# A two-block layer on one core: sixteen buffers for expert tiles instead of twelve, and the filter, its spectra and the embedding product inside the expert stage

## The chip, the core and the metric

The kernel runs on one core of a Trainium2 chip. The metric is the device time of one execution in microseconds (us). TensorE (PE in the profile) multiplies, VectorE (DVE) and ScalarE (ACT) compute elementwise and bring results out of PSUM, GpSimd (POOL) does a few tiny operations, and SyncE (SP) issues nearly all transfers. The engines run their own instruction streams and wait for one another by semaphores.

## The reference

`x` is 256 tokens by 1024 channels. The reference is two blocks, one after the other:

```python
# block 1
x = x + hybrid_mixer(rms_norm(x), ...)          # state space mixer and attention
x = x + hier_moe(rms_norm(x), ...)              # 32 experts, 2 of them for each token
gate = sigmoid(rms_norm(x) @ w_ple_gate)        # 1024 x 1024
x = x + gate * (p @ w_ple)                      # p: 256 x 256, w_ple: 256 x 1024
x = rms_norm(x)
# block 2
proj = rms_norm(x) @ w_in_2                     # hyena branch, attention branch, gates
k_spec = hyena_filter_spectra(L, w_f1, ..., w_f3)   # depends on weights and positions only
...                                             # long convolutions with k_spec, attention
x = x + merged @ w_out_2
```

and of it

```python
def hier_moe(...):          # per expert, d = 1024, f = 256
    hid = silu(h @ w_gate[e]) * (h @ w_up[e])
    out += comb[:, e] * (hid @ w_down[e])
def hyena_filter_spectra(...):
    h = sin(freq_1 * (z @ w_f1 + b_f1)); h = sin(freq_2 * (h @ w_f2 + b_f2))
    k = (h @ w_f3) * decay                      # 256 x 2048
    return rfft(concat(k[:, :, 0], k[::-1, :, 1]))
```

`p @ w_ple` and `k_spec` depend on nothing that is computed before them.

## The kernel before

**Dense products.** The weights of the dense products come as tiles of up to 128 x 2048 words (1 MB) through four raw buffers (`raw`). ACT copies a tile into a high part (`WH`, L1022), DVE subtracts it from the raw tile for a low part (`WL`, L1438), in three slots each, and PE multiplies high and low parts in three passes (`gemm`, `mul3`). Every PE product is issued by one of two helpers, L469 (`mul`) and L478 (`turn`, a transpose), so nearly all PE rows carry these lines. A product of float32 operands shows as two matmul rows in the profile, one of the split kind as one row each pass.

**The expert stage.** The 32 experts are done four at a time, in eight rounds `q` = 0 to 7. Each round has twelve tiles of 1 MB: four `w_gate`, four `w_up`, four `w_down`, 96 in all. They are not split but used as float32. PE does in a round, in this order: `first(q, 0)` (gate, 32 products that go to four column strips of one PSUM bank), `first(q, 1)` (up), `slots`, for q < 6 two gathers of token rows for the next pair of rounds, `scatter(q - 1)`, `hidden_T`, `down(q)`. The outputs are scaled (ACT L1259, DVE L1958) and the scatter adds them to four PSUM banks that stay open through the stage. With the two banks of `down` that leaves two of the eight banks (`ring.of`) for everything else in the stage. `Ring.take` makes PE wait, before it writes a bank again, for the engine that reads the bank's last contents.

**Buffers of the stage.** The tiles go to twelve buffers in turn (`held`): the four raw buffers, the six halves of the `WH` and `WL` slots, a part of `arena`, and `XN`. Tile t + 12 is fetched into the buffer of tile t as soon as the whole set of four that tile t belongs to has been multiplied (`fetch_expert`). All fetches stand in one queue, SP's, in the order in which the program writes them, and an entry that waits holds up everything behind it. After the first twelve tiles SP issues the constants of block 2 (`cst2`, 1952 KB; `w_f3_2`, 512 KB; two small matrices; `p`, 256 KB; the final norm's weight, 512 KB), then tiles 12 to 95, then the tiles of the dense weights `w_ple` (2 of 0.5 MB), `w_ple_gate` (4) and block 2's.

**The filter.** Its two small layers run at the ends of rounds 2 and 3. The eight products with `w_f3_2` (`kf`, 64 rows deep, 512 columns; DVE multiplies each by the decay, L1926) run four at the end of round 6 and four at the end of round 7. The spectra (eight steps `ks`, two float32 products of 128 x 128 x 512 each) are filler work after the stage: steps 0 and 1 after the product with `w_ple`, 2 and 3 after the transposes of the next norm, 4 to 7 after the product with `w_ple_gate`. Two steps make a pair: ACT copies the first one's bank, and DVE forms the difference and the sum with the second (L1485 or L1487, L1490).

**After the stage.** DVE splits the first three weight tiles, adds the scattered sums to `X` (L1982), and PE transposes `p`, multiplies it by `w_ple` (24 split products), transposes the normed `X` (`rows_T("np")`), multiplies by `w_ple_gate` (96 split products). The result is gated and added, two norms follow, `rows_T("ng")`, and block 2's products.

Of the kernel before, what the change touches and what calls it, by code (L numbers as in the profile page):

```python
# [12 lines left out]
ALU = mybir.AluOpType  # L13
# [6 lines left out]
NRAW = 4  # L20
# [4 lines left out]
NEXP = 12  # L25
# [139 lines left out]
def program(nc, A, out):  # L165
    ctx = ExitStack()
    with ctx:
# [8 lines left out]
        d_expert = [signal(f"d_e{i}") for i in range(NEXP)]  # L176
# [105 lines left out]
        iota, hyb = C["iota"], arena[0:1, 4096:5120]  # L282
# [21 lines left out]
        KI = arena[:, 6144:8192].rearrange("p (f d) -> p f d", f=2)  # L304
        PX = arena[:, 8192:10240].rearrange("p (t d) -> p t d", t=2)
# [5 lines left out]
        FH = arena[0:64, 10240:10752].rearrange("p (a l) -> p a l", a=2)  # L311
        PT_ = tuple(x[:, 0:512].rearrange("p (c l) -> p c l", c=2) for x in HD_)
        SG = sg_[:, :].rearrange("p (a l) -> p a l", a=2)
        FGU = arena[:, 4096:8192].rearrange("p (c n) -> p c n", c=8)
        FD = arena[:, 8192:10240].rearrange("p (c n) -> p c n", c=2)
# [9 lines left out]
        KQ = arena[:, 8192:9728].rearrange("p (t d) -> p t d", t=2)  # L325
        V2 = arena[:, 9728:10752].rearrange("p (t d) -> p t d", t=2)
# [61 lines left out]
        filled_from = dense_again % NRAW  # L388
        slots_in_order = [(dense_again + i) % NSPLIT for i in range(NSPLIT)]
# [3 lines left out]
        moe_set = lambda t: (("gate", "up", "down")[t // 4 % 3], t // 12)  # L393
        slot_emptied = {s: moe_set(96 - NEXP + NRAW + 2 * i + 1) for i, s in enumerate(slots_in_order)}
        for key, w, kc in (("wpl", wpl, 2), ("wpg", wpg, 8)):
            for i in range(2):
                weight((key, i), w, kc, 512 * i, 512)
# [31 lines left out]
        class Splitting:  # L429
# [5 lines left out]
            def due(self, consumed):  # L435
                while self.k < self.end:
                    before = tiles[self.k]["before"]
                    if before is not None and before >= consumed:
                        return
                    self.k += 1  # L440
                    yield self.k - 1
# [22 lines left out]
        def tensor(e):  # L464
# [34 lines left out]
            def fill(n):  # L499
                for name, c in todo.next(n):  # L500
                    if name == "spectra":
                        spectrum(c)
                        continue
# [234 lines left out]

            def first(q, m):
                if m == 0:  # L740
# [1626 lines left out]
```

## Time and profile before

| | us |
|---|---|
| median of three runs | 935.06 (933.81 to 940.55) |
| the profiled execution | 934.24, span 932.4 |
| PE busy | 777.8 (83% of the span) |
| DVE busy | 473.8 (51%) |
| ACT busy | 333.8 (36%) |
| expert tiles on their way | from 323 to 606 of the span |

The span is the part of the execution between the first and the last recorded instruction; the 1.8 us left are outside it. The page gives the engines' busy shares in 40 slices of 23.3 us; the chain of waits says what ended last, step by step.

### The profile page before, as it was taken

The page shows a single profiled execution, that of the slowest core. Times are in us where ns is not written, and L with a number is a line of the kernel's source. Part 1 is how long each engine was busy: PE and PEld are TensorE (multiplying, and loading weights), DVE is VectorE, ACT ScalarE, POOL GpSimd, SP SyncE. Part 2 cuts the span into 40 slices and gives each one's busy share as a digit, 9 for nine tenths or more (in the row PEclk, how much of TensorE's full clock was granted, in tenths as well). Part 3 has the DMA queues.
Part 4 walks back from the last instruction along what each step waited for, and adds up shares of the span by engine and source line. Part 5 has one row for each costly group of instructions (what it writes and reads, how often), then busy time and mean ns, then how long its engine had stood idle before and what let it go on. Part 6 is the DMA issues. An engine that isn't in the chain of part 4 may idle for free.

```text
span 932.4 us, 10988 instructions
## 1 busy us (share of the span) xinstructions
PE 777.8 (83%) x4611; PEld 583.8 (63%) x4611; DVE 473.8 (51%) x797; ACT 333.8 (36%) x485; POOL 20.3 (2%) x16
## 2 busy tenths in 40 slices
PE   3999799979989984677776676769799989999978
PEld 3988677757768873533343342337499866578766
DVE  5678755554675555311212111255575668755662
ACT  5454344545543235111101010034445452346620
POOL 0000000000000000000000000000000004100000
PEclk8999899889999998789888998879999999999999
DMA  7645551122442448699999999962236663242401
GB/s 255 199 171 187 174 181 46 46 91 90 136 136 82 156 153 339 227 422 420 421 422 421 420 421 421 415 230 90 69 99 203 199 209 115 68 158 91 135 1 45
DMA packets 62890, 190.30 MB, mean 204 GB/s; under 512 B 7633, under 2 KB 11955, under 8 KB 50356
## 3 DMA queue, kind: packets, MB, share of 16 engines
q1 hardware_dynamic: 61826, 187.01, 54.1%
q10 hardware_dynamic: 1010, 2.54, 0.7%
q8 instruction: 38, 0.62, 0.3%
q14 instruction: 16, 0.13, 0.0%
HBM read 188.49 MB, written 1.05 MB: 203 GB/s over the span
## 4 chain that ended last, share of the span: by engine, by line
PE 60%; DMA 18%; DVE 12%; ACT 6%; SPq 2%; issue 1%; POOL 0%; DVEq 0%; ACTq 0%
PE pb L469 58%; DMA WLo<-in_w_exp_up 14%; DVE WL L1438 3%; DMA XN<-in_w_exp_down 3%; ACT WH L1022 3%; PE pb L478 2%; SPq L2278 1%; DMA arena<-in_b_short 1%; ACT arena L1052 1%; DVE cv_ L1560 1%; SPq L2262 0%; ACT arenao L1225 0%; DVE arena L1502 0%; ACT L1052 0%; DVE XN L1445 0%
## 5 line engine op out<-in xcount | busy, mean ns | idle before, releaser
L1438 DVE TENSOR_TENSOR WL<-raw,WH 128x2048 fp32r<-128x2048 f32 (+5 forms) x82 | 176.5, 2166 | 124.7 <-ACT WH L1022 124.6
L469 PE MATMUL pb<-WH,HTh 128*128 128x512 f32 (+2 forms) x464 | 189.9, 409 | 22.3 <-DVE HTl L1465 7.8
L1022 ACT ACTIVATE WH<-raw 128x2048 fp32r<-128x2048 f32 (+5 forms) x82 | 147.1, 1805 | 150.8 <-PE pb L469 150.8
L469 PE MATMUL pb<-WH,HTl 128*128 128x512 f32 (+2 forms) x464 | 181.5, 391 | 0.0
L469 PE MATMUL pb<-WL,HTh 128*128 128x512 f32 (+2 forms) x464 | 181.5, 391 | 0.0
L469 PEld LDWEIGHTS pb<-WH,HTh 128*128 128x128 f32 x464 | 89.1, 192 | 48.5 <-issue 7.7
L469 PEld LDWEIGHTS pb<-WL,HTh 128*128 128x128 f32 x464 | 88.9, 192 | 18.3
L469 PEld LDWEIGHTS pb<-WH,HTl 128*128 128x128 f32 x464 | 89.3, 192 | 16.8 <-issue 1.2
L1941 DVE TENSOR_TENSOR rt_<-rt_,pb 128x256 f32<-128x256 f32 x8 | 3.4, 421 | 122.7 <-ACT rt_ L1249 122.7
L469 PE MATMUL pb<-arena 128*128 128x512 f32 (+6 forms) x188 | 63.1, 469 | 3.0 <-DVE arena L1926 2.2
L469 PE MATMUL pb<-WLo,arena 128*32 128x256 f32 x256 | 45.9, 498 | 19.4 <-DMA WLo<-in_w_exp_up 19.4
L469 PE MATMUL pb<-WHo,arena 128*32 128x256 f32 x256 | 48.0, 501 | 12.4 <-DMA WHo<-in_w_exp_up 12.4
L469 PE MATMUL pb<-raw,arena 128*32 128x256 f32 x512 | 41.2, 432 | 16.1 <-DMA raw<-in_w_exp_gate 15.0
L469 PE MATMUL pb<-HTh,WH 128*128 128x256 f32 (+1 forms) x184 | 53.4, 290 | 0.3 <-DVE HTl L1469 0.3
L469 PE MATMUL pb<-HTh,WL 128*128 128x256 f32 (+1 forms) x184 | 53.0, 288 | 0.0
L469 PE MATMUL pb<-HTl,WH 128*128 128x256 f32 (+1 forms) x184 | 53.0, 288 | 0.0
L1249 ACT ACTIVATE rt_<-pb 128x256 f32<-128x256 f32 x8 | 3.1, 383 | 126.9 <-PE pb L469 126.9
L469 PE MATMUL pb<-arena,rt_ 128*128 128x64 f32 (+1 forms) x160 | 43.5, 415 | 5.8 <-DVE rt_ L1475 5.8
L469 PEld LDWEIGHTS pb<-arena 64*128 64x128 f32 (+4 forms) x188 | 30.5, 191 | 26.8 <-issue 18.5
L469 PEld LDWEIGHTS pb<-WLo,arena 128*32 128x32 f32 x256 | 19.9, 141 | 43.2 <-DMA WLo<-in_w_exp_up 26.0
L469 PEld LDWEIGHTS pb<-raw,arena 128*32 128x32 f32 x512 | 19.2, 124 | 38.9 <-DMA raw<-in_w_exp_gate 20.2
L478 PE MATMUL pb<-c,arena 128*128 128x128 f32 (+2 forms) x200 | 28.9, 281 | 13.5 <-DMA arena<-in_b_short 4.7
(308 smaller groups left out, 1180.9 us busy)
## 6 DMA issues: line engine op xcount, KB each, us to landing
raw<-in_w_in SPq DMA_DIRECT2D x46, 1024.0 KB, 5.1
raw<-in_w_exp_gate SPq DMA_DIRECT2D x32, 1024.0 KB, 20.4
WHo<-in_w_exp_up SPq DMA_DIRECT2D x16, 1024.0 KB, 16.9
WLo<-in_w_exp_up SPq DMA_DIRECT2D x16, 1024.0 KB, 19.3
raw<-in_w_out SPq DMA_DIRECT2D x8, 1024.0 KB, 5.4
WHo<-in_w_exp_down SPq DMA_DIRECT2D x8, 1024.0 KB, 16.8
WLo<-in_w_exp_down SPq DMA_DIRECT2D x8, 1024.0 KB, 18.9
arena<-in_w_exp_down SPq DMA_DIRECT2D x8, 1024.0 KB, 20.6
```

The source lines that it names most:

```text
L469: return e.matmul(o, l, r, start=start, stop=stop, skip_group_check=True)
L478: return e.transpose(o, i, ident[0:k, 0:k])
L1022: e.activation(h_, r_, ACT.Copy).then_inc(hi.sem, hi.mark(k))
L1052: e.activation(dst[:, t, :], pb((name, t))[:, 0:n], f).then_inc(ac.sem, ac.mark((name, t)))
L1249: e.activation(HG[q % 2], pb(("gu", q))[:, 0:256], ACT.Silu).then_inc(ac.sem, ac.mark(("su", q)))
L1438: e.tensor_tensor(l_, r_, h_.bitcast(F32), ALU.subtract).then_inc(lo.sem, lo.mark(k))
L1560: e.scalar_tensor_tensor(out=cv[:, s:L], in0=u[:, 0:L - s], scalar=cw[:, 3 - s, g:g + 1], in1=cv[:, s:L], op0=ALU.mult, op1=ALU.add).then_inc(
L1941: e.tensor_tensor(HG[q % 2], HG[q % 2], pb(("gu", q))[:, 256:512], ALU.mult).then_inc(ve.sem, ve.mark(("gu", q)))
L2278: e.dma_start(held[i], w).then_inc(d_expert[i].sem, d_expert[i].mark(("x", t), by=16))
```

## The change

- **Sixteen buffers** for the first tiles (`NHELD`). Four of them, parts of `arena`, hold one tile each only (buffers 0, 1, 5, 7); from tile 16 on twelve buffers turn, and three of those (6, 9, 10) are given up during round 6. Which tile goes where is worked out ahead by a small table.
- The first sixteen tiles and tiles 16 to 27 stand in SP's queue **before** the constants of block 2, `p`, the final norm's weight and, new there, `hy_bias_2`, which ACT issued in round 5.
- `w_ple` is one float32 tile more in the stage's stream (97 tiles), ahead of round 7's. `p` is transposed at the end of round 2. The product is eight float32 products (`side_product`) at the start of round 7, two for each half of the columns and each half of the tokens, on the two free banks.
- All eight `kf` products stand at the end of **round 5**, and all eight steps of the spectra at the end of **round 6**. ACT's and DVE's part of them moves along.
- The weights' tiles start with `w_ple_gate`. The first of them is split by ACT after round 7 and by DVE inside the norm, between its sum and its scaling; the next two after the norm's high and low parts.
- The fallback for tokens that no slot takes uses other addresses; it is not entered.

The core of the diff:

```diff
-NEXP = 12
+NHELD = 16
...
-        held = ([raws[(filled_from + i) % NRAW] for i in range(NRAW)] + [x[:, s, :] for s in slots_in_order
-                for x in (WHf, WLf)] + [arena[:, 8192:10240], XN.rearrange("p t d -> p (t d)")])
+        held = [arena[:, 16896:18944], arena[:, 10752:12800], *last_raw[0:3], arena[:, 12800:14848],
+                arena[:, 8704:10752], arena[:, 14848:16896], last_raw[3],
+                *[x[:, s, :] for s in emptied for x in (WHf, WLf)], XN.rearrange("p t d -> p (t d)")]
+        held_once, held_until = (0, 1, 5, 7), {6: 79, 9: 81, 10: 82}
+        moe_tiles = []
+        for q in range(8):
+            moe_tiles += [("wpl",)] if q == 7 else []
+            moe_tiles += [(m, q, g) for m in ("gate", "up", "down") for g in range(4)]
+        ring, buffer_of, held_before, held_last = deque(), {}, {}, {}
+        for t, name in enumerate(moe_tiles):
+            i = t if t < NHELD else ring.popleft()
+            buffer_of[name], held_before[name] = i, held_last.get(i)
+            held_last[i] = name
+            if i not in held_once and t < held_until.get(i, len(moe_tiles)):
+                ring.append(i)
...
@@ tensor
+            def kernel_rows(n):
+                o = ring.take(("kf", n), ve)
+                ac.wait_ge(e, ("fh", 1))
+                mul(o[:, :], FH[:, 1, (n // 4) * 128:(n // 4) * 128 + 128],
+                    FW[:, (n % 4) * 512:(n % 4) * 512 + 512]).then_inc(mm.sem, mm.mark(("kf", n)))
...
+            def side_product(i, t):
+                o = ring.take(("px", i, t), (ve, ac)[t])
+                ac.wait_ge(e, "pT")
+                w = held_tile(("wpl",), 2)
+                for c in range(2):
+                    ins = mul(o[:, :], PT_[:, c, t * 128:t * 128 + 128], w[:, c, 512 * i:512 * i + 512], c == 0, c == 1)
+                ins.then_inc(mm.sem, mm.mark(("px", i, t), *([("wpl",)] if i and t else [])))
...
             for q in range(8):
-                first(q, 0)
-                first(q, 1)
+                if q == 7:
+                    for i in range(2):
+                        for t in range(2):
+                            side_product(i, t)
+                first(q, "gate")
+                first(q, "up")
...
-                if q >= 6:
-                    for n in range(4 * (q - 6), 4 * (q - 6) + 4):
...
+                if q == 5:
+                    for n in range(8):
+                        kernel_rows(n)
+                if q == 6:
+                    for s in range(8):
+                        spectrum(s)
...
-            for i in range(2):
-                gemm(("wpl", i), ("wpl", i), PT_, "pT", (ve, ac))
-            fill(2)
             rows_T("np")
-            fill(2)
             for i in range(2):
                 gemm(("wpg", i), ("wpg", i), HT, "np", (ac, ac))
-            fill(99)
             rows_T("ng")
...
@@ vector
-            def norm_rows(n, src):
+            def norm_rows(n, src, split_to=None):
                 norm_sum(n, src)
+                if split_to:
+                    weights(None, split_to)
                 po.wait_ge(e, ("rs", n))
...
@@ sync
-            for t in range(NEXP):
-                fetch_expert(t)
-            mm.wait_ge(e, ("mT", "T", 6))
-            ve.wait_ge(e, ("x mix", 1))
+            for t in range(28):
+                fetch_held(t)
+            mm.wait_ge(e, ("up", 0))
             e.dma_start(c2[:, 0:A["cst2"].shape[1]], A["cst2"]).then_inc(d_c2.sem, d_c2.mark("in", by=16))
...
-            for t in range(NEXP, 96):
-                fetch_expert(t)
+            for t in range(28, len(moe_tiles)):
+                fetch_held(t)
```

PE's instructions from the end of `down(6)` on (names `pb0` to `pb7` are PSUM banks; `arena` holds the filter's rows; `raw`, `WHo`, `WLo`, `XN` hold expert tiles). Before, two of the round's `kf` products run freely, the other two wait, and round 7 follows:

```order
L469 MATMUL pb6<-arena,rt_ 32x512
L469 MATMUL pb6<-XN,rt_ 32x512
L469 MATMUL pb7<-arena 128x512
L469 MATMUL pb0<-arena 128x512
L469 MATMUL pb7<-arena 128x512 [waits s_ve]
L469 MATMUL pb0<-arena 128x512 [waits s_ve]
```

With the change, in the same place:

```order
L485 MATMUL pb6<-WHo,rt_ 32x512
L485 MATMUL pb0<-arena 128x512 x2
L485 MATMUL pb7<-arena 128x512 x2
L485 MATMUL pb0<-arena 128x512 [waits s_ve]
L485 MATMUL pb0<-arena 128x512
L485 MATMUL pb7<-arena 128x512 x2
...
L485 MATMUL pb0<-WLo,arena 128x512 [waits d_e12,s_ve]
L485 MATMUL pb0<-WLo,arena 128x512
L485 MATMUL pb7<-WLo,arena 128x512 x2
L485 MATMUL pb0<-WLo,arena 128x512 [waits s_ve]
L485 MATMUL pb0<-WLo,arena 128x512
L485 MATMUL pb7<-WLo,arena 128x512 [waits s_ac]
L485 MATMUL pb7<-WLo,arena 128x512
L485 MATMUL pb0<-WHo,arena 32x256 [waits d_e13,s_ve]
```

Four pairs of spectra steps, each after the first with a wait for DVE, and the eight products with `w_ple` (its tile in `WLo`) now stand between `down(6)` and the first product of round 7.

SP's queue from the first tiles on, before:

```order
L2278 DMA arena<-in_w_exp_down 128x2048 [waits s_ve]
L2278 DMA XN<-in_w_exp_down 128x2048 [waits s_ve,s_mm]
L2313 DMA arena<-in_cst 128x3904
L2317 DMA arena<-in_w_f_2 64x2048
...
L2318 DMA arena<-in_final_norm_w 128x1024
L2278 DMA raw<-in_w_exp_gate 128x2048 [waits s_mm]
```

and with the change:

```order
L2313 DMA XN<-in_w_exp_gate 128x2048 [waits s_ve,s_mm]
L2313 DMA raw<-in_w_exp_up 128x2048 [waits s_mm]
L2313 DMA raw<-in_w_exp_up 128x2048
L2313 DMA raw<-in_w_exp_up 128x2048 [waits s_mm]
L2313 DMA arena<-in_w_exp_up 128x2048
...
L2313 DMA XN<-in_w_exp_gate 128x2048
L2348 DMA arena<-in_cst 128x3904
L2352 DMA arena<-in_w_f_2 64x2048
```

The constants stood behind tile 11, the first one into `XN`; now they stand behind tile 27, the second one into `XN`, which waits for round 1's gate products.

DVE at the norm after the stage, before:

```order
L1441 TENSOR_SCALAR small<-small 128x2 [waits s_ve,s_ac]
L1454 TENSOR_SCALAR XN<-X,small 128x1024 [waits s_po]
L1438 TENSOR_TENSOR WL<-raw,WH 128x2048 [waits s_hi]
L1475 COPY arena<-pb 128x512 [waits s_mm]
L1438 TENSOR_TENSOR WL<-raw,WH 128x2048 [waits s_hi]
```

and with the change:

```order
L1469 TENSOR_SCALAR small<-small 128x2 [waits s_ve,s_ac]
L1466 TENSOR_TENSOR WL<-raw,WH 128x2048 [waits s_hi]
L1484 TENSOR_SCALAR XN<-X,small 128x1024 [waits s_po]
L1499 SCALAR_TENSOR_TENSOR HTl<-pb,small,HTh 128x256 [waits s_ac]
```

One tile's split moved ahead of the scaling; the other splits, the copies and the spectra's sums left this place.

## Rows read from the trace of the kernel before

**Rows 1.** The page: tenths of full clock and of DMA time, 40 slices.

```profile
PEclk8999899889999998789888998879999999999999
DMA  7645551122442448699999999962236663242401
```

**Rows 2.** Busy time in stretches: us, PE, PEld, DVE, ACT, POOL, PEclk, DMA share, GB/s.

```profile
380.00:390.00 10.00, 7.90 (x62) 7.16 (x64) 3.42 (x8) 3.18 (x5) 0.00 (x0) 0.68 0.49 120
540.00:580.00 40.00, 28.83 (x259) 14.45 (x251) 5.31 (x16) 3.72 (x8) 0.00 (x0) 0.91 1.01 421
```

**Rows 3.** The chain that ended last: start, us, what (L469 is any product).

```profile
542.58 23.78 DMA WLo<-in_w_exp_up
566.40 5.75 PE pb L469 x58
...
576.36 3.69 PE pb L469 x32
...
581.99 24.23 DMA XN<-in_w_exp_down
606.26 3.63 PE pb L469 x26
```

**Rows 4.** Instructions of SP's queue in order of time: start, us, line, operation.

```profile
371.29 0.43 SPq L2313 DMA_DIRECT2D arena<-in_cst  x1
...
392.27 1.99 SPq L2278 DMA_DIRECT2D raw<-in_w_exp_gate  x4
...
404.37 0.33 SPq L2278 DMA_DIRECT2D WHo<-in_w_exp_down  x1
```

**Rows 5.** A DMA issue line: count, KB each, median us from issue to landing.

```profile
raw<-in_w_out SPq DMA_DIRECT2D x8, 1024.0 KB, 5.4
```

**Rows 6.** Matmuls in order of time, rounds 0, 6 and 7: start, us, shapes.

```profile
388.55 3.66 PE L469 MATMUL pb<-raw,arena 128*32 128x256 f32 x64 [1.08 <-DVE arena L1918]
...
579.93 1.98 PE L469 MATMUL pb<-arena 64*128 64x512 f32 x4
582.91 1.12 PE L469 MATMUL pb<-arena 64*128 64x512 f32 x2 [1.00 <-DVE arena L1926]
584.29 2.06 PE L469 MATMUL pb<-arena 64*128 64x512 f32 x2 [0.26 <-DVE arena L1926]
```

**Rows 7.** A stretch as in Rows 2, at half clock.

```profile
584.33:591.16 6.83, 6.83 (x50) 2.80 (x54) 1.87 (x3) 0.00 (x0) 0.00 (x0) 0.50 1.01 422
```

**Rows 8.** Matmuls in order of time, after the stage.

```profile
632.52 3.59 PE L469 MATMUL pb<-arena 128*128 128x512 f32 x8
635.95 1.94 PE L478 MATMUL pb<-c,XN 128*128 128x128 f32 x16
...
663.07 7.03 PE L469 MATMUL pb<-arena 128*128 128x512 f32 x16
```

**Rows 9.** ACT in order of time, after the stage.

```profile
641.49 0.60 ACT L1064 ACTIVATE arena<-pb 128x512 f32<-128x512 f32 x1 [1.83 <-PE pb L469]
```

**Rows 10.** The same view of DVE.

```profile
610.70 1.41 DVE L1958 SCALAR_TENSOR_TENSOR HDl<-pb,small,HDh 128x512 fp32r<-128x512 f32 x2 [6.67 <-ACT HDh L1259]
...
615.39 4.55 DVE L1438 TENSOR_TENSOR WL<-raw,WH 128x1024 fp32r<-128x1024 f32 x3
619.86 2.48 DVE L1982 TENSOR_TENSOR X<-pb,X 128x512 f32<-128x512 f32 x4
624.63 0.69 DVE L1465 TENSOR_TENSOR HDl<-pb,HDh 128x512 fp32r<-128x512 f32 x1 [2.30 <-issue]
625.24 1.22 DVE L1445 CUSTOM_DVE_ANT_0 XN<-X 128x1024 f32<-128x1024 f32 x1
...
627.56 0.75 DVE L1454 TENSOR_SCALAR XN<-X,small 128x1024 f32<-128x1024 f32 x1 [0.81 <-POOL small L2234]
632.00 2.29 DVE L1438 TENSOR_TENSOR WL<-raw,WH 128x2048 fp32r<-128x2048 f32 x1 [3.69 <-ACT WH L1022]
...
642.85 0.69 DVE L1490 TENSOR_TENSOR arena<-arena,pb 128x512 f32<-128x512 f32 x1
```

More of the change, by code:

```diff
@@ L1 @@
 import math
+from collections import deque
 from contextlib import ExitStack, nullcontext
@@ L439, in due, with until @@
                         return
+                    self.k += 1
+                    yield self.k - 1
+            def until(self, n):
+                while self.k < n:
                     self.k += 1
@@ L1012, in scalar, with weights @@
             todo = Steps()
-            def weights(consumed):
-                for k in splitting.due(consumed):
+            def weights(consumed, end=None):
+                for k in splitting.until(end) if end else splitting.due(consumed):
                     h_, _, r_ = tile_flat(k)
@@ L1247, in scalar @@
             for q in range(8):
+                if q == 7:
+                    for i in range(2):
+                        mm.wait_ge(e, ("px", i, 1))
+                        e.activation(PX[:, 1, 512 * i:512 * i + 512], pb(("px", i, 1))[:, :], ACT.Copy).then_inc(
+                            ac.sem, ac.mark(("px", i, 1)))
                 mm.wait_ge(e, ("up", q))
@@ L1263, in scalar @@
                     e.activation(FH[:, 1, :], FH[:, 0, :], ACT.Sin).then_inc(ac.sem, ac.mark(("fh", q - 2)))
-                if q == 5:
-                    e.dma_start(hyb, A["hy_bias_2"].rearrange("a o n -> a (o n)")).then_inc(
-                        d_hyb.sem, d_hyb.mark("in", by=16))
+                if q == 2:
+                    mm.wait_ge(e, "pT")
+                    e.activation(PT_, pb("pT")[:, :].rearrange("p (c l) -> p c l", c=2), ACT.Copy).then_inc(
+                        ac.sem, ac.mark("pT"))
+                if q == 6:
+                    for c in range(1, 8, 2):
+                        _, _, o_, _ = SPECTRA[c]
+                        mm.wait_ge(e, ("ks", c))
+                        e.activation((KR, KI)[c // 4][:, 0, o_ * 512:o_ * 512 + 512], pb(("ks", c - 1))[:, :],
+                                     ACT.Copy).then_inc(ac.sem, ac.mark(("ks", c)))
             splitting.end = len(tiles)
-            weights(dense_again)
+            weights(None, dense_again + 1)
             with e.If(e.value_load(flag[0:1, :], min_val=0, max_val=1) > 0):
@@ L1283, in scalar @@
                 e.wait_ge(fve.sem, fve.after(e, ("x", 31)))
-            todo.add("spectra", 8)
-            high("pT", PT_, 2, after=("sc", 7))
             norm_rows("np", X, after="x moe")
-            for i in range(2):
-                weights(used(("wpl", i)))
-                drain_t((("wpl", i), 1), PX[:, 1, 512 * i:512 * i + 512])
-            fill(2)
             high("np", HT, 8, pnw)
-            fill(2)
+            weights(dense_again)
             for i in range(2):
@@ L1432, in vector, with weights @@
             todo = Steps()
-            def weights(consumed):
-                for k in splitting.due(consumed):
+            def weights(consumed, end=None):
+                for k in splitting.until(end) if end else splitting.due(consumed):
                     h_, l_, r_ = tile_flat(k)
@@ L1972, in vector @@
                     sine(("fh", n), FH[:, 1, :], FH[:, 0, :], FH[:, 1, :], FH[:, 0, :], False)
-                if q >= 6:
-                    for n in range(4 * (q - 6), 4 * (q - 6) + 4):
+                if q == 5:
+                    for n in range(8):
                         kernels(n)
+                if q == 6:
+                    for c in range(1, 8, 2):
+                        spectrum(c)
             splitting.end = len(tiles)
-            weights(dense_again)
             for t in range(2):
@@ L1999, in vector @@
                     e.wait_ge(fve.sem, fve.after(e, ("x", x)))
-            todo.add("spectra", 8)
-            low("pT", PT_, 2)
             ve.wait_ge(e, "x moe")
-            norm_rows("np", X)
-            for i in range(2):
-                weights(used(("wpl", i)))
-                drain_t((("wpl", i), 0), PX[:, 0, 512 * i:512 * i + 512])
-            fill(2)
+            norm_rows("np", X, dense_again + 1)
             low("np", HT, 8, pnw)
-            fill(2)
+            weights(dense_again)
             for i in range(2):
```

182 lines of the change are left out of this document (88 added, 94 removed).

## The prediction

> **What bounds the kernel now.** I read the page first, for its slices of clock and DMA [rows 1]. A slice is 23.3 us; in slices 18 to 26 (396 to 606 us) the DMA stands at nine tenths or more, so in the expert stage the transfers bound. The stretch 540 to 580 us says it in numbers [rows 2]: 421 GB/s, and PE busy 28.8 of 40 us, so PE has 11.2 us to spare in 40, about one round. At 421 GB/s a tile of 1 MB takes 2.49 us.
>
> The chain of waits then gives the end of the stage [rows 3]: `up(6)` waits for its last tile until 566.40, `down(6)` ends at 576.36 + 3.69 = 580.05, and the last product, `down(7)`, waits until 606.26 for a tile issued at 581.99. That landing, **T = 606.26**, is the point from which I count. SP's queue tells how the stream starts [rows 4]: the constants (3.2 MB) are issued at 371.29, right behind the first twelve tiles, and tile 12 only at 392.27, when `gate(0)` is done. Between them the DMA is half idle: 120 GB/s in 380 to 390 us [rows 2]. So the constants cost the stream nothing today.
>
> Behind T I read PE, ACT and DVE in order of time [rows 8 to 10]: the scaled outputs are ready at 610.70 + 1.41 = 612.1, DVE is then held by decays and by 4.55 us of splits, the additions to `X` end at 622.34, the transposes of the norm start at 635.95, and the product with `w_ple_gate` ends at 663.07, T + 56.8. The spectra and the product with `w_ple` stand between and cost PE time on this path.
>
> **The change, part by part, as T' against T.**
>
> *Stream.* Four tiles more lie ahead: 4 x 2.49 = 10.0 us gained. The 3.2 MB of constants move from half-idle DMA time into the full stretch: 3.26 MB at 421 GB/s is 7.8 us lost, up to 9.6 with `hy_bias_2` and short rows; I take 8.8. `w_ple` is one more tile ahead of round 7: 2.5 us lost. After tile 15 only tiles 16 to 19 can be issued before `down(0)` is done (SP issued behind it at 404.37 [rows 4]): 10 us of work in the 12 us from 392.3 on, so a gap of 0 to 4 us, taken as 2.1. Sum: T' = T + 3, about **609.7, if the transfers still bound**. The next step says that they don't.
>
> *`kf` to the end of round 5.* Four products before take 579.93 to 586.35 with DVE's waits, the single pair 1.12 us at full and 2.06 us at half clock [rows 6]. The first two run freely (1.98), and from 582.91 to 584.29 a further one takes 1.38 us with its wait: eight take 2.0 + 6 x 1.38 = 10.3 us, and with half clock in all of them some 2.0 + 6 x 2.1 = 14.6. They are covered by PE's spare time of a round, 11.2 us. So they make round 6 0 to 3.4 us late; I take `down(6)` ending at 582.5 instead of 580.05.
>
> *Spectra to the end of round 6.* In round 7 the same spare time is used: `gate(7)` now waits for them. A pair of steps is 3.59 us of PE [rows 8]. Only two banks are free (order of PE above), and the next pair waits for DVE: ACT copies at 641.49 for 0.60, and DVE's second pass ends at 642.85 + 0.69 = 643.54 [rows 9, 10], 2.05 us behind PE's end at 641.49, with the semaphore 2.2. Four pairs: 4 x (3.59 + 2.2) = **23.2 us**. After the stage these pauses cost nothing, since other products stood between.
>
> *The clock there.* In 584.33 to 591.16 the granted clock was 0.50 with PE busy all 6.83 us [rows 7], that is 1.2 of 2.4 GHz, right behind the stretch in which PE paused for tiles and for the decays [rows 6]. The four pauses of 2.2 us may set it off again. The ends: nothing, and all four pairs at half clock, 4 x 3.6 = 14.4 us. Nearest is the one such stretch of 6.8 us, in which 3.4 us are lost, beside pauses of like length: I take 2.5. By the Trainium skill ("TensorE: Matmul & The Clock Gate", "A second HAM failure mode: psum-queue depth-cycling"), cycling through PSUM banks with a micro-idle between groups makes the clock swing again and again; the four pairs on two banks are such a case. By that rule the sum would stand nearer the upper end, T' some 10 us later; it is a rival below. The same page ("Why this matters for your kernels") says that only long idle gaps between bursts lose the clock; by it this term is nothing.
>
> *Product with `w_ple`.* Eight float32 products of 128 x 128 x 512; a product is two matmul rows, and sixteen rows of this shape took 7.03 [rows 8], so **7.0 us**. ACT and DVE empty its banks in 0.6 and 0.69 against 1.8 for the two products of the next bank: hidden. The 24 split products after the stage go.
>
> *`gate(7)` and the last tiles.* A gate set is 3.66 us [rows 6]. The last three tiles (`down(7)`, 94 to 96) go to the buffers of `gate(7)`'s first three tiles, and can be issued only when `gate(7)` is done. Today they reuse buffers of round 6. The queue is empty by then, so the landing is 5.4 us for the first [rows 5] and 2 x 2.49 for the others: **10.4 us**. `up(7)`, `slots` and `hidden_T` lie beside it.
>
> Sum: T' = 582.5 + 23.2 + 2.5 + 7.0 + 3.7 + 10.4 = **629.3, which is T + 23.0**. PE, not the DMA, sets it.
>
> *Behind T'.* From the last landing to the scaled outputs 5.85 us as now (612.11 - 606.26). The scatter is eight products, 3.6 us; the four additions 2.48 [rows 10]. No decay and no split stands ahead of them: they end at T' + 12.0, before at T + 16.1, so -4.1. From there to the transposes: 2.30 for the semaphore, some 1.5 for the sum, 2.29 for the split that moves in ahead of the scaling, and 0.75, together 6.9; before it was 13.6 because of the product with `w_ple` and the first pair of spectra, so -6.7. From the transposes to `w_ple_gate` 1.94 + some 1.5 for copying out = 3.5; before 641.49 - 635.95 = 5.5, with a pair between: -2.0. The product itself stays, 21.6. Together **-12.8**. Its weights are issued behind tile 96 and land from T' + 2.5 to T' + 10. The second tile's low part is ready about when the first tile's products end; its cover is thin, and 1 to 2 us could be lost. The eight spectra products of 7.03 us behind `w_ple_gate` were hidden under the norms [rows 8], so their removal is worth nothing.
>
> Net: +23.0 - 12.8 = +10.2. The profiled execution was 934.24 and its span 932.4, with 1.8 outside it in both; 934.24 + 10.2 = 944.4, and the median shown is 0.8 higher than this execution: **945**.
>
> **Rivals.**
>
> *Warm clock and a free round 5.* With no clock term and `kf` wholly covered, T' is 2.5 + 2.5 us earlier, so 940, and 938 where the pair's wait comes out shorter than 2.2 us by 0.5. For it: `kf` has a cover of 11.2 us [rows 2]. Against: the clock fell at just this place [rows 6, 7]. 0.17.
>
> *Half clock through the spectra and the `w_ple` product.* Up to 14.4 - 2.5 = 11.9 us more: 950 to 957. For it: pauses of 2 us between bursts of 3.6; against: in 540 to 580 us PE was idle for 11.2 us and the mean clock still 0.91 [rows 2]. 0.12. This is what the depth-cycling rule of the Trainium skill's page would give.
>
> *The transfers still bound, and the kernel is faster.* If PE's inserted work found cover, T' were 609.7 and the time 934.24 + 3.4 - 12.8 + 0.8 = 926. PE has 11.2 us per round to spare, and a lead of four tiles might let PE work ahead; but the inserted work in rounds 5 to 7 is 10 + 23 + 7 = 40 us against spare time of three rounds, 34, and the last three tiles' buffers are tied to `gate(7)`, so the lead can't be used at the end. It decides if the pairs need under about 3 us each. I give 0.08; a partial case (T' about 615 to 620, 931 to 936) gets 0.03.
>
> **Chances.** The forecast has 0.60, with a range of its own of 941 to 950. One per cent of 935.06, about what a measurement can tell from no change, is 9.4: faster is below 925.7 and slower above 944.4. The forecast's half above 944.4 gives 0.31, its rest 0.29; with the rivals: slower 0.31 + 0.12 = 0.43, same 0.29 + 0.17 + 0.03 = 0.49, faster 0.08. The range 936 to 951 leaves out the faster rival, the partial case and most of the half-clock one, some 0.2.
>
> **What would show it.** In the profile after: `down(6)` ends near 582; four bursts of 3.6 us with waits of 2.2 us for DVE between them, then eight products of `w_ple`; DMA falls from its nine tenths to a few tenths between 600 and 620 us; `gate(7)` ends near 619 and `down(7)` waits until 629 for the tile into `raw` or a half slot, 10 us later; the transposes of the norm start 19 us behind that; behind the `w_ple_gate` product PE has nothing of the filter. It would be wrong if the last tile lands before 615 (PE's work was covered), if PE's clock in 583 to 620 is 0.5 or 1.0 throughout, or if DVE's moved split or a late `w_ple_gate` tile takes back a part of the 12.8 us. The constants' issue, moved to about 409 us, would show a round 1 or 2 that waits some 10 us for tiles.

## The result

| | median, us | ratio to the kernel before | 95% interval |
|---|---|---|---|
| before | 935.15 | | |
| changed | 952.30 (950.63 to 954.57) | 1.0174 | 1.0129 to 1.0219 |
| changed, once more beside the last experiments | 951.69 (before there: 938.53) | 1.0137 | 1.0120 to 1.0154 |

The change makes the kernel 13 to 17 us slower. The forecast was 945, with a range of 936 to 951: its centre and its main mechanism pointed the right way, the size was too small. (Its chances gave 0.43 to slower and 0.49 to no change that could be told.) The profiled execution took 952.04 with a span of 950.2, 17.8 us above that of before.

The page of the changed kernel, clock and DMA in 40 slices of 23.8 us, as in [rows 1]:

```profile
PEclk9999899989989996895798889897779989999989
DMA  7646351123432686399999999284225553142401
```

The DMA falls to 2 in slice 26 (594 to 618 us), where it stood at 9 before (583 to 606 us there). In that slice PE does the spectra and the product with `w_ple`. The chain that ended last, as in [rows 3], shows it:

```profile
581.21 7.29 PE pb L485 x40
588.51 0.60 ACT arena L1301
589.14 0.70 DVE arena L1963
589.87 0.70 DVE arena L1966
590.61 3.71 PE pb L485 x8
...
602.27 5.41 PE pb L485 x8
...
609.80 12.43 PE pb L485 x80
...
623.09 9.19 DMA XN<-in_w_exp_down
632.33 3.63 PE pb L485 x26
```

The 40 products from 581.21 are `down(6)` and the first pair. Behind each pair PE waits for ACT and two passes of DVE; the last tile is issued at 623.09 and lands at 632.33, where it landed at 606.26 before. PE's own rows give the sizes, with half clock in a part of the fourth pair (5.40 for 3.70) and of the eight products with `w_ple` (8.79 for 7.0). Matmuls in order of time:

```profile
584.78 3.70 PE L485 MATMUL pb<-arena 128*128 128x512 f32 x8
590.61 3.70 PE L485 MATMUL pb<-arena 128*128 128x512 f32 x8 [2.13 <-DVE arena L1966]
596.44 3.70 PE L485 MATMUL pb<-arena 128*128 128x512 f32 x8 [2.13 <-DVE arena L1966]
602.27 5.40 PE L485 MATMUL pb<-arena 128*128 128x512 f32 x8 [2.13 <-DVE arena L1966]
609.80 8.79 PE L485 MATMUL pb<-WLo,arena 128*128 128x512 f32 x16 [2.13 <-DVE arena L1966]
```

and the stretches, with the columns of [rows 2]. PE was busy 17.5 of 26 us while the DMA moved 256 GB/s; in the second stretch the DMA moved nothing:

```profile
584.00:610.00 26.00, 17.48 (x41) 6.54 (x34) 6.91 (x10) 3.65 (x6) 0.00 (x0) 0.93 0.62 256
609.80:618.50 8.70, 8.70 (x16) 3.60 (x16) 1.38 (x2) 0.60 (x1) 0.00 (x0) 0.81 0.00 0
```

The kernel is 26.1 us late at 632.33. How much of it is left later is read best from one operation that both kernels have. ACT's split of a `w_ple_gate` tile that stood at 647.00 before is 12.4 us late; so 13.7 us came back, by the shorter way into that product. ACT's first split behind block 2's first products, at 686.60 before, is **16.0 us late**, and the end 17.8. The 3.6 us between the two are a loss that I had not forecast. At the entry of block 2 PE's rows are:

```profile
689.19 3.68 PE L494 MATMUL pb<-c,XN 128*128 128x128 f32 x16 [13.55 <-ACT XN L1063]
694.91 0.55 PE L485 MATMUL pb<-HTh,WH 128*128 128x256 f32 x1 [2.04 <-DVE HTl L1499]
```

Before, in the same view:

```profile
676.78 3.47 PE L478 MATMUL pb<-c,XN 128*128 128x128 f32 x16 [6.68 <-ACT XN L1031]
680.52 0.36 PE L469 MATMUL pb<-HTh,WH 128*128 128x256 f32 x1 [0.27 <-DVE HTl L1469]
```

Two things differ: PE idles 13.55 us instead of 6.68 ahead of the transposes, and behind them it waits 2.04 us for DVE instead of 0.27. The experiments tell these apart. Both readings come with half clock in the transposes (3.47 and 3.68 us for sixteen, 1.94 at full clock [rows 8]), so the clock had fallen before the wait for DVE began.

### The profile page after: what moved, and what is told of

It is laid out like the page before. It is cut to its first block, busy times and chain, and to the rows that moved or that the text cites. A ratio compares the mean times of both kernels' runs of the same rounds, so it can differ in the third digit from the quotient of the medians.

```text
span 950.2 us, 10962 instructions
## 1 busy us (share of the span) xinstructions
PE 781.0 (82%) x4603; PEld 585.7 (62%) x4603; DVE 471.9 (50%) x794; ACT 332.7 (35%) x483; POOL 22.2 (2%) x16
## 4 chain that ended last, share of the span: by engine, by line
PE 64%; DVE 13%; DMA 11%; ACT 7%; issue 2%; SPq 2%; POOL 1%; DVEq 0%; ACTq 0%; POOLq 0%
PE pb L485 61%; DMA arena<-in_w_exp_up 10%; DVE WL L1466 3%; ACT WH L1054 3%; PE pb L494 3%; SPq L2313 1%; DMA XN<-in_w_exp_down 1%; ACT HTh L1078 1%; ACT arena L1084 1%; POOL small L2261 1%; DVE XN L1473 1%; DMA X<-in_x 1%; DVE cv_ L1576 1%; ACT XN L1063 0%; DVE arena L1685 0%
## 5 line engine op out<-in xcount | busy, mean ns | idle before, releaser
L1466 DVE TENSOR_TENSOR WL<-raw,WH 128x2048 fp32r<-128x2048 f32 (+5 forms) x80 | 174.2, 2189 | 122.8 <-ACT WH L1054 122.7
L1054 ACT ACTIVATE WH<-raw 128x2048 fp32r<-128x2048 f32 (+5 forms) x80 | 145.1, 1824 | 151.3 <-PE pb L485 151.3
L485 PE MATMUL pb<-arena 128*32 128x256 f32 (+5 forms) x364 | 100.5, 453 | 16.5 <-DMA arena<-in_w_exp_up 7.0
L485 PEld LDWEIGHTS pb<-arena 128*32 128x32 f32 (+3 forms) x364 | 46.8, 158 | 57.1 <-issue 25.4
L485 PE MATMUL pb<-XN,arena 128*32 128x256 f32 (+2 forms) x208 | 57.6, 440 | 6.5 <-DMA XN<-in_w_exp_gate 5.6
L485 PE MATMUL pb<-raw,arena 128*32 128x256 f32 x400 | 47.6, 435 | 14.2 <-DMA raw<-in_w_exp_up 14.1
L485 PE MATMUL pb<-WLo,arena 128*32 128x256 f32 (+1 forms) x224 | 47.0, 515 | 11.9 <-DMA WLo<-in_w_exp_gate 5.6
L494 PE MATMUL pb<-c,XN 128*128 128x128 f32 x128 | 23.5, 349 | 38.5 <-ACT XN L1063 38.5
L494 PEld LDWEIGHTS pb<-c,XN 128*128 128x128 f32 x128 | 21.1, 197 | 40.9 <-ACT XN L1063 29.2
L485 PEld LDWEIGHTS pb<-XN,arena 128*32 128x32 f32 (+1 forms) x208 | 28.7, 163 | 23.5 <-issue 13.1
```

The lines of the kernel that those rows point to most:

```text
L485: return e.matmul(o, l, r, start=start, stop=stop, skip_group_check=True)
L494: return e.transpose(o, i, ident[0:k, 0:k])
L1054: e.activation(h_, r_, ACT.Copy).then_inc(hi.sem, hi.mark(k))
L1466: e.tensor_tensor(l_, r_, h_.bitcast(F32), ALU.subtract).then_inc(lo.sem, lo.mark(k))
```

## The experiments

Times of a row are medians; ratios are to the kernel before on the same chip, whose median was 938.0 in the first four experiments, 938.4 in the next four and 938.5 in the last. These are three chips, so a difference between two groups is best taken from the ratios.

**1. The spectra back.** The changed kernel with

```diff
-                if q == 6:
-                    for s in range(8):
-                        spectrum(s)
+            # steps 0, 1 before rows_T("np"), 2, 3 behind it,
+            # 4 to 7 behind the product with w_ple_gate
```

(and the buffer of the `w_ple` product moved to the room of the late spectra). ACT and DVE follow.

> The changed kernel with the eight steps of the spectra where the kernel before has them: two before the transposes of the norm after the stage, two behind them, four behind the product with w_ple_gate. Sixteen buffers, SP's order, kf at the end of round 5 and the w_ple tile and product stay. My theory: the 25.0 us that PE spends in four pairs of steps between down(6) and the w_ple product push the last tile's landing out; without them the transfers bound again, the last product's wait ends at 609.5 instead of 632.3 (-22.8), a pair in the norm costs 3.7 again, and the 5.4 us lost in block 2 come back: 952.3 - 24.5 = 928, range 924 to 932. Rival, the reuse of gate(7)'s buffers and the constants in the full stretch are what delays the last tile: then it lands after 618 and the time is 936 or more.

Measured: 933.63, ratio 0.9949 (0.9928 to 0.9969). The stage's cause is confirmed: 18 to 21 us below the changed kernel by one move, where 24.5 were expected. But 928 was missed by 5. The last product starts at 614.85 and not at 609.5, since the stream of tiles is later than the sum had it (see below). A second part is again the entry of block 2, where idle time was as before and the loss was there all the same:

```profile
673.13 3.68 PE L494 MATMUL pb<-c,XN 128*128 128x128 f32 x16 [6.68 <-ACT XN L1067]
679.57 0.55 PE L485 MATMUL pb<-HTh,WH 128*128 128x256 f32 x1 [2.75 <-DVE HTl L1511]
```

That speaks against idle time as the sole cause: from the transposes to ACT's first split the trace loses 5.1 us against the kernel before, more than the changed kernel's 3.6.

**2. Half of it.** Steps 0 to 3 at the end of round 6, 4 to 7 behind `w_ple_gate`.

> The changed kernel with steps 0 to 3 of the spectra at the end of round 6 and steps 4 to 7 behind the product with w_ple_gate. My theory: two pairs less in the stage give 2 x 5.83 = 11.7 us, the half clock behind them up to 3 more, and the eight products behind w_ple_gate keep PE's clock up into block 2, 5.4 us: 934, range 931 to 938. Rival, the loss in block 2 has nothing to do with these products: 940.

Measured: 934.61, ratio 0.9966 (0.9942 to 0.9990). In its trace the last tile is waited for until 617.09 instead of 632.33: 15.2 us for two pairs. 11.7 of them are the pairs, the rest is clock: the pairs that are left take 3.70 each, and the product with `w_ple` 7.13 instead of 8.79. The number fell where it was expected, but not for the whole reason given: the trace still loses 3.1 us at the entry of block 2, behind a wait of 1.19 us, where nothing was to be lost.

**3. Useless products.** Behind `w_ple_gate`:

```diff
+            for j in range(2):
+                o = ring.take(("dummy", j), mm)
+                for n in range(8):
+                    ins = mul(o[:, :], C["fc"][:, 0:128], KR[:, 0, 0:512])
+                ins.then_inc(mm.sem, mm.mark(("dummy", j)))
```

> The changed kernel with sixteen useless matmuls of 128x128x512 (7 us of PE) behind the product with w_ple_gate, where the kernel before has steps 4 to 7 of the spectra; nobody reads their results. Theory clock: PE is idle 13.6 us before the transposes of block 2's norm in the changed kernel and 6.7 in the one before, and the first products of block 2 run at half clock until 698; with the idle time back at 6.7 us the loss behind w_ple_gate, 5.4 us, comes back: 947, range 945 to 949. Rival, block 2's weights or DVE's order are late: the products change nothing, 952.

Measured: 947.45, ratio 1.0107 (1.0078 to 1.0137). The text misjudged its own edit: sixteen float32 products are 32 rows, and they filled PE for 13.89 us, up to the transposes. The number fell where the clock theory put it, but its interval overlaps that of the changed kernel (1.0120 to 1.0154), and the trace shows a wait of 3.06 us for DVE:

```profile
672.50 13.89 PE L485 MATMUL pb<-arena 128*128 128x512 f32 x32
686.23 2.03 PE L494 MATMUL pb<-c,XN 128*128 128x128 f32 x16
691.32 0.36 PE L485 MATMUL pb<-HTh,WH 128*128 128x256 f32 x1 [3.06 <-DVE HTl L1504]
```

The transposes run at full clock (2.03 for 3.68), and what they win is lost in a longer wait. The profiled execution was also 3 us ahead already at 629.39, before the products, and indeed at the start of `gate(0)` (387.31 against 390.16), so only part of its 5.6 us of span under the changed kernel is theirs.

This trace shows one thing more. Its four pairs are those of the changed kernel, in the same place, and the clock falls in the second, is back in the third, and falls in the fourth:

```profile
585.88 5.40 PE L485 MATMUL pb<-arena 128*128 128x512 f32 x8 [2.13 <-DVE arena L1971]
593.40 3.70 PE L485 MATMUL pb<-arena 128*128 128x512 f32 x8 [2.13 <-DVE arena L1971]
599.24 5.40 PE L485 MATMUL pb<-arena 128*128 128x512 f32 x8 [2.14 <-DVE arena L1971]
```

**4. Before without the late filler.** Steps 4 to 7 of the spectra are left out.

```diff
-            todo.add("spectra", 8)
+            todo.add("spectra", 4)
```

> The kernel before with steps 4 to 7 of the spectra left out of the computation (their outputs stay unwritten), on PE, ACT and DVE; nothing else differs. Theory clock: less work makes it slower by the loss seen in block 2 of the changed kernel, 3.6 to 5.4 us: 939.5, range 938 to 941. Rival, those products were only hidden work: 934 to 935.5.

Measured: 940.44, ratio 1.0022 (1.0001 to 1.0043): 2 us more for less work, half of what was expected, and an interval that nearly touches no change. In the trace PE idles 13.55 us ahead of the transposes, and the first product waits 2.05 us for DVE. Since leaving steps out also turns the ring of banks, this run can't tell the two causes apart.

**The ring of banks.** The four runs showed waits of 2.75, 1.19, 3.06 and 2.05 us at the same place. `Ring.take` gives the banks in turn, so a step moved or left out moves every later user. PE's instructions at this place in the program's order, banks by number, before:

```
L469 MATMUL pb4<-arena 128x512 x2
L478 MATMUL pb5<-c1,XN 128x128 [waits s_ve,s_ac]
L478 MATMUL pb5<-c1,XN 128x128 x3
L478 MATMUL pb6<-c1,XN 128x128 x4
L478 MATMUL pb7<-c1,XN 128x128 x4
L478 MATMUL pb0<-c1,XN 128x128 x4
L469 MATMUL pb1<-HTh,WH 128x256 [waits s_lo,s_ve]
```

and in the changed kernel:

```
L494 MATMUL pb0<-c1,XN 128x128 [waits s_ve,s_ac]
L494 MATMUL pb0<-c1,XN 128x128 x3
L494 MATMUL pb1<-c1,XN 128x128 x4
L494 MATMUL pb2<-c1,XN 128x128 x4
L494 MATMUL pb3<-c1,XN 128x128 x4
L485 MATMUL pb0<-HTh,WH 128x256 [waits s_ve,s_lo]
```

The first product takes four banks at once. Before they are 1 to 4, and the transposes' banks 5, 6, 7, 0, so PE begins as soon as the first chunk is ready. With the change they are the transposes' own four, and PE waits for the last of DVE's passes over them. The orders of the other kernels agree: where the last of the transposes' banks is among the four it waited 2.05 to 3.06 us (experiments 1, 3, 4), where only their first two are, 1.19 us (experiment 2).

**5. Other banks, nothing else.** The changed kernel with

```diff
+            ring.i = 4
             rows_T("ng")
+            ring.i = 0
```

> The changed kernel with one thing else: the sixteen transposes of block 2's norm go to PSUM banks 4 to 7 instead of 0 to 3. Theory banks: in the changed kernel block 2's first product takes banks 0 to 3 and waits 2.04 us until DVE has emptied the transposes' banks, while in the kernel before the ring stood eight banks further and it found them free (wait 0.27); so the wait falls under 0.5 and the first products reach full clock earlier: 1.9 to 3.6 us faster than the changed kernel, 949.5. Rival clock alone: the idle time of 13.6 us before the transposes decides, the banks do not: the gain is under 1 us.

Measured: 946.98, ratio 1.0089 (1.0062 to 1.0115), against 1.0137 (1.0120 to 1.0154) for the changed kernel: 4.7 us between the medians, 4.5 by the ratios, since the two ran on different chips. (The expectation has the ring of the kernel before eight banks further; the listing above is right.) The idle time ahead is the same 13.55, and the wait is gone:

```profile
689.12 3.68 PE L494 MATMUL pb<-c,XN 128*128 128x128 f32 x16 [13.55 <-ACT XN L1063]
692.46 0.56 PE L485 MATMUL pb<-HTh,WH 128*128 128x256 f32 x1
```

The stretches 689 to 696 and 696 to 700 us of this kernel, and behind them those of the changed one:

```profile
689.00:696.00 7.00, 6.88 (x36) 6.88 (x37) 4.84 (x9) 3.43 (x9) 0.00 (x0) 0.58 0.00 0
696.00:700.00 4.00, 4.00 (x36) 4.00 (x35) 2.86 (x2) 0.35 (x1) 0.00 (x0) 1.00 0.51 144
```

```profile
689.00:696.00 7.00, 4.77 (x21) 4.40 (x22) 4.78 (x9) 3.49 (x9) 0.00 (x0) 0.50 0.00 0
696.00:700.00 4.00, 4.00 (x26) 4.00 (x26) 2.92 (x2) 0.00 (x0) 0.00 (x0) 0.69 0.48 136
```

PE does 36 matmuls instead of 21 in the first, and stands at full clock from 696 on while the changed kernel has 0.69. The trace of the mended kernel is 2.9 us ahead at ACT's first split (699.65 against 702.57): the wait, and an earlier rise of the clock. A second gain of 2.6 us follows some 60 us later. There both kernels wait 3.19 us for DVE, and the stretches behind are, of the changed kernel and of the mended one:

```profile
764.60:770.60 6.00, 6.00 (x20) 6.00 (x21) 1.28 (x4) 0.05 (x1) 0.00 (x0) 0.53 0.56 178
```

```profile
761.80:767.80 6.00, 6.00 (x37) 6.00 (x36) 2.75 (x5) 1.44 (x2) 0.00 (x0) 1.00 0.54 178
```

The same pause is followed by 0.53 of full clock in one and by full clock in the other. The kernel before drops there too, for about 3 us. So this part of the gain depends on when the pause falls, and belongs to the bank order only by way of the timing.

**6. The reverse.** The kernel before, filler and all, with transposes and first products on the same banks:

```diff
+            ring.i = 20
             fill(99)
             rows_T("ng")
+            ring.i = 24
```

> The kernel before with all its filler work, but the transposes of block 2's norm and its first products both on PSUM banks 0 to 3 (the four late steps of the spectra on 4 to 7). Theory banks: a wait of about 2 us for DVE appears ahead of the first product, and half clock behind it: 2 to 3.5 us slower than the kernel before. Rival clock alone: the filler still keeps PE busy until 670, so no change (under 0.7 us).

Measured: 941.12, ratio 1.0027 (1.0011 to 1.0044), 2.5 us by the ratio. The wait appears with PE idle only the usual 6.68 us ahead, and the trace loses 4.3 us from the transposes to ACT's first split:

```profile
677.62 3.39 PE L478 MATMUL pb<-c,XN 128*128 128x128 f32 x16 [6.68 <-ACT XN L1033]
684.21 0.55 PE L469 MATMUL pb<-HTh,WH 128*128 128x256 f32 x1 [3.20 <-DVE HTl L1471]
```

The clock takes part here as well. It was full again when the wait began, fell with it, and stayed at half for 3 us behind it. In the stretches 681 to 684 and 684 to 687 us PE does nothing, and then works at half clock:

```profile
681.00:684.00 3.00, 0.01 (x1) 0.00 (x0) 3.00 (x9) 1.05 (x3) 0.00 (x0) 1.00 0.01 3
684.00:687.00 3.00, 2.79 (x13) 2.82 (x14) 3.00 (x2) 0.00 (x0) 0.00 (x0) 0.50 0.00 0
```

The rival that the clock decides and the banks do not falls in both directions. All the traces read at this place agree. From the transposes to ACT's first split they lose, against the kernel before, 3.6 us in the changed kernel, 5.1, 3.1, 2.8 and 3.3 in experiments 1 to 4 and 4.3 in this one, each with a wait; experiment 5 and the kernel of experiment 12 have none and lose 0.7 and 0.5. The loss isn't in proportion to the wait (2.75 us cost 5.1, 3.06 cost 2.8): the rest is when the clock falls and rises.

**7. Spectra back and other banks**, experiments 1 and 5 in one.

> The changed kernel with the spectra where the kernel before has them and with the bank order of the last two texts (transposes of block 2's norm on banks 4 to 7). It lost 5.0 us between w_ple_gate and block 2's weights against the kernel before when only the spectra went back. Theory banks: 3 to 5 us below the kernel with the spectra back alone, that is 8 to 10 us below the kernel before. Rival: the wait comes from DVE's order of work and not from the banks, then no gain over it, 4 to 5 us below the kernel before.

Measured: 931.92, ratio 0.9937 (0.9915 to 0.9958), 6 us below before and about 1 us below experiment 1, not told apart from it. The expected 8 to 10 us were not reached. The bank order that cured experiment 5 did a new harm: the transposes now share banks 4 to 7 with the late spectra, and wait for DVE there (8.71 us idle instead of 6.68).

**8. Twelve buffers.** As 7, with

```diff
-NHELD = 16
+NHELD = 12
-            for t in range(28):
+            for t in range(NHELD):      # the constants stand behind these
```

> As the last kernel, but with twelve buffers for expert tiles again and the constants of block 2 issued right behind the twelfth tile, in the time in which the DMA is idle (hy_bias_2 behind tile 27). Theory stream: sixteen buffers gain 10 us and the constants' move into the full stretch, the gap before down(0) and the slow short rows take 14 to 16 back; with twelve the last product can start near 608.8 (606.3 and one tile for w_ple) instead of 614.9: 5 to 7 us below the last kernel, 13 to 16 below the kernel before. Rival: the four tiles ahead are worth more than the constants cost, then it is slower than the last kernel by up to 3 us.

Measured: 930.53, ratio 0.9917 (0.9894 to 0.9939), with an interval that overlaps that of 7. The last product starts at 609.38 instead of 612.77, 3.4 us earlier, and not the 5 to 7 expected.

**9. The changed kernel once more.**

> The changed kernel itself once more, unchanged, beside the others on this chip, so that the gain of the bank order is read against it: 16 to 17 us above the kernel before, as at first (ratio 1.0174). Rival: the first comparison lay high and it is 12 to 14 us, near the 8 to 10 of the two kernels that only mended its way into block 2.

Measured: 951.69, ratio 1.0137, between the two readings; the first interval (1.0129 to 1.0219) holds it.

**10. The pairs behind `up(7)`.** The same work on PE in another place:

```diff
                 first(q, "up")
+                if q == 7:
+                    for s in range(8):
+                        spectrum(s)
```

> The changed kernel with its four pairs of spectra steps between up(7) and slots(7) instead of before round 7. Same work on PE, but gate(7) is done before the pairs, so the last three tiles can be fetched while PE does them. Theory PE-bound: between down(6) and the last product stand 25 us of pairs, 7 to 8.7 of w_ple, and the sets of round 7, and the fetch behind gate(7) adds only what up(7), slots and hidden_T do not cover (1.4 us of wait in the profile): 1 to 4 us below the changed kernel. Rival, the tie of the last tiles to gate(7)'s buffers costs the 10.4 us that the prediction had for it: 6 or more below.

Measured: 959.38, ratio 1.0221 (1.0202 to 1.0240). Both theories missed: it is slower than the changed kernel by 7.7 us. PE now waits for `up(7)`'s last tile until 604.00, and only then do the pairs start:

```profile
604.00 0.63 PE L485 MATMUL pb<-WHo,arena 128*32 128x256 f32 x1 [1.87 <-DMA WHo<-in_w_exp_up]
...
611.36 3.67 PE L485 MATMUL pb<-arena 128*128 128x512 f32 x8 [1.02 <-DVE rt_ L1973]
...
641.42 0.62 PE L485 MATMUL pb<-WLo,rt_ 128*32 128x512 f32 x1 [0.52 <-DVE rt_ L1986]
```

Where the change has them, the pairs stand beside transfers that PE would wait for anyhow. So a part of the 25 us is covered there, and none here.

**11 and 12. Versions that beat both.** Spectra back, and banks in the order of the kernel before, each one number lower (`ring.i = 4` behind `scatter(7)`), which the expectations take for the same; 11 with twelve buffers, 12 with sixteen.

> Twelve buffers with the constants behind the twelfth tile, kf at the end of round 5, w_ple tile and product in the stage, spectra as in the kernel before, and the banks after the stage taken in the order of the kernel before (w_ple_gate on 4 to 7, late spectra on 0 to 3, transposes of block 2's norm on 4 to 7, block 2's first products on 0 to 3). The kernel with twelve buffers so far lost 2.0 us at the transposes, which waited for DVE (8.71 us idle instead of 6.68): 2 us below it, 9 to 12 us below the kernel before. Rival: the late spectra then wait for ACT instead and nothing is gained.

> As the last one, with the change's sixteen buffers and SP order. In the traces the last tile of up(7) came at 602.2 with sixteen and at 600.2 with twelve. Theory stream: sixteen buffers are worth less than what the constants cost in the full stretch, 1 to 3 us above the last kernel. Rival: no difference or a gain.

Measured: 929.85, ratio 0.9917 (0.9902 to 0.9932), and 928.60, ratio **0.9893** (0.9877 to 0.9908). The best is 10 us below the kernel before and 23 below the change. It keeps the change's buffers, its tile order, `kf` in round 5 and the `w_ple` product in the stage. In 12 the last product starts at 613.51 and nothing is waited for at block 2:

```profile
613.51 0.62 PE L485 MATMUL pb<-WLo,rt_ 128*32 128x512 f32 x1 [0.52 <-DVE rt_ L1996]
...
672.10 3.68 PE L494 MATMUL pb<-c,XN 128*128 128x128 f32 x16 [6.68 <-ACT XN L1068]
675.84 0.55 PE L485 MATMUL pb<-HTh,WH 128*128 128x256 f32 x1
```

With twelve the last product starts 4.3 us earlier in the trace (609.18), and yet the time is not shorter: the intervals overlap. The twelve-buffer kernel idles 4.88 us behind the scatter in its profile, put down to issue; why was not found.

## Why the prediction was wrong, step by step

**The step that failed** is the last one of "Behind T'": the eight late products of the spectra "were hidden under the norms, so their removal is worth nothing". As PE work they were hidden. But they were also two pairs in the ring of banks, and moving them, with the `w_ple` product, turned the ring so that block 2's first product took the transposes' banks. I priced instructions and their DVE passes, and not which bank the next one gets, though the order of the changed kernel, with bank numbers, was there to read. The step measured 5.4 us in the trace (17.8 at the end against 12.4 in `w_ple_gate`). Without it the other errors, 3.0 us at T' and 0.9 back, would have left some 947, inside the range (an estimate from the table below). Experiment 5, which changes the bank alone, gives 4.7 us back by its medians, and 6.2 in the trace (span 944.0), of which 2.6 hang on where a later pause falls. Its trace ends 11.6 us late, against 12.4 in `w_ple_gate`: with the banks free the removal was indeed worth nothing. By its ratio this kernel is 8.4 us above the one before, where the forecast had 9.9; that the two come so near is in part luck, since its last tile is about 3 us later than forecast, too.

The others, prediction against profile:

| step | predicted | measured |
|---|---|---|
| `down(6)` ends | 582.5 | 584.8 |
| four pairs, with the clock | 25.7 | 25.0 (584.78 to 609.80) |
| product with `w_ple` | 7.0 | 8.7 |
| `gate(7)` | 3.7 | 3.7 (next tile issued at 622.24) |
| to the last landing | 10.4 | 10.1 |
| T' | 629.3 | 632.33 |
| from T' into `w_ple_gate` | -12.8 | -13.7 |
| behind it | 0 | +5.4 |

- **Which engine bounds** was right: the DMA is idle from 600 on (17 GB/s in 600 to 610, of the 421 of [rows 2]). The wait behind a pair is 2.13 us against 2.2.
- **`down(6)`** ended 2.3 us later than forecast. 1.6 us of it stood already at the start of `gate(0)` (390.16, before 388.55 [rows 6]), ahead of all that the sum has; the other traces start it between 387.3 and 390.4. `kf` took 11.8 us (555.82 to 567.6), between the 10.3 and 14.6 given; ten of its sixteen rows in one piece of 7.40 show half clock. Its cover was misread: a round is 12 tiles of 2.49 us, 29.9 us and not 40, so PE has 8.4 us to spare in one, not 11.2, and 25 in three, not 34. How the last 0.7 us divides between `kf`, its cover and the stream is open.
- **The clock** cost 1.7 us in the fourth pair and 1.7 in the `w_ple` product, where I had 2.5 for the pairs alone. The depth-cycling section of the Trainium skill's page "TensorE: Matmul & The Clock Gate" would have had it swing again and again. In the changed kernel three of four pairs ran at full clock with pauses of 2.13 us between them. But the same pairs swing in experiment 3, where the second and the fourth took 5.40, and in experiments 5 and 10 it was the third. So the swings exist, at 1.7 us each, and the 10 us that the prediction gave to that rule were too much. Experiment 6 shows the same at block 2, a clock that falls with a pause for a bank and costs more than the pause; in the changed kernel it had fallen before, and rose later.
- **Adding the pairs up** as PE time was right for forecasting a stage that PE bounds. Taking them away (changed kernel, 632.33; experiment 12, 613.51) moves the last product by 18.8 us and not by 25.0, since the chain then runs from `up(7)`'s last tile, which lands at 602.70. Experiment 10 shows the covered part from the other side.
- **The tie to `gate(7)`'s buffers** was sized well as a piece of the chain (10.1). What undoing it alone is worth is not shown: experiment 10 takes it off the path, but moves the pairs to where nothing covers them.
- **The stream** was sized too small. The last tile of `up(5)`, from which on PE bounds, lands 5.5 us later than before, here the changed kernel's chain and below it that of before:

```profile
517.54 23.19 DMA arena<-in_w_exp_up
540.77 5.34 PE pb L485 x58
```

```profile
512.15 23.12 DMA WLo<-in_w_exp_up
535.31 5.93 PE pb L469 x58
```

Less the 1.6 us ahead of `gate(0)` that is 3.9 us, where I forecast a net loss of 0.9 for buffers and constants. The gap before `down(0)` was there (238 GB/s from 405 to 410 us, before 419), and 430 to 445, when the constants were on their way, ran at 351 GB/s, before 419. With the constants behind the twelfth tile (experiment 11) the same tile lands at 534.85. So the 609.7 of the sum, "if the transfers still bound", was too early by some 4 us: experiment 12 starts the last product at 613.51. In time, experiments 7 and 8, and 11 and 12, find no difference that their intervals tell from nothing.

- **The faster rival** had its condition right: with the spectra out of the stage the change wins. Its 926 was too low; the same parts give 933.63 in experiment 1 and 928.60 with the banks put right, beside 938.0 and 938.5 for the kernel before.

## What to carry to other kernels

Filler work that moves leaves two holes: its time and its place in every rotation (banks, slots, buffers) behind it. After such a move, list which bank each of the next takers gets and who drains it. Work of an engine that waits between pieces belongs where other work stands between the pieces; price it by the piece and the drain, and see which transfers it hides before it is moved.

## What was not expected of the hardware

- A wait of 2.04 us for a bank cost 2.9 us up to ACT's next split: the granted clock, at half since the transposes, rose at 698 to 699 us and without the wait at 695. In experiment 6 a wait of 3.20 us cost 4.3, and the clock fell behind it.
- A pause of 3.19 us was followed by 5 to 6 us near half clock in the changed kernel, in both of its profiles, by about 3 in the kernel before, and by none in the kernel of experiment 5, which differs from the changed one by its banks alone. What of the earlier work decides it stayed open.
- In four equal pairs with pauses of 2.13 us the clock fell in the fourth (the changed kernel, twice), in the third (experiments 5 and 10) or in the second and fourth (experiment 3), with nothing in the rows that sets them apart. With two pairs (experiment 2) it fell in none.
- Adding 13.89 us of useless products made the changed kernel no slower: 947.45 against 951.69, the two measured beside the same kernel before at 938.0 and 938.5.
